# Results scattered by token rows and read back by plain loads, overflow blocks ahead of expert 29, roots and roundings of ScalarE ahead at the seam

## The reference, cut to what matters

```python
g_idx = argmax(xt @ w_gr + b_gr)                       # one of 4 groups per token
top_v, top_i = top_k(e_logits_of_that_group, 2)        # 2 of its 8 experts
wts = g_prob * softmax(top_v)
for each expert e of 32:                               # its tokens, xb
    y = (silu(xb @ w_gate[e]) * (xb @ w_up[e])) @ w_down[e]
h = h + sum over the token's two experts of wts * y    # 1024 result rows in all
h = rms_norm(h, final_gain)                            # then adaln and the convolution mixer
```

## Time and profile before

| | |
|---|---|
| time, median of 3 runs | 1503.96 us (1501.43 to 1504.95) |
| the profiled execution, its own time | 1503.66 us |
| its span, first to last instruction | 1501.9 us |
| mean granted TensorE clock | 0.985 |
| PE busy | 1409.8 us (94%) |
| DVE, ACT, POOL busy | 699.5, 486.0, 43.5 us |
| expert stage, first `up` to last `result` | 275.5 to 756.0 us |
| seam, PE without its own work until | 779.5 us |

### The profile page before, as it was taken

How to read it: one execution, slowest core, us unless ns; L and a number is a source line. 1 busy time by engine, 2 the same in 40 slices (tenths; PEclk the granted TensorE clock), 3 DMA queues, 4 the chain that set the end, 5 groups by cost and what they waited for, 6 DMA issues and landing times.

```text
span 1501.9 us, 18075 instructions
## 1 busy us (share of the span) xinstructions
PE 1409.8 (94%) x6944; PEld 984.8 (66%) x6944; DVE 699.5 (47%) x1311; ACT 486.0 (32%) x739; POOL 43.5 (3%) x75
## 2 busy tenths in 40 slices
PE   6999998999998888999859999999999999999997
PEld 5877677544433333343248888788888888888886
DVE  5377656611110111110077657466266566666555
ACT  6463335011100000111063221334344444444552
POOL 2001000000000000000120000000000000000000
PEclk9999899999999999999979999999999999999999
DMA  8827435699999998999985455202213122112101
GB/s 357 359 79 268 157 141 207 264 423 425 426 427 426 427 427 341 387 427 426 426 305 213 170 206 196 92 21 89 110 57 113 57 72 98 57 56 105 64 15 57
DMA packets 36809, 336.84 MB, mean 224 GB/s; under 512 B 4560, under 2 KB 4688, under 8 KB 18384
## 3 DMA queue, kind: packets, MB, share of 16 engines
q1 hardware_dynamic: 29632, 304.69, 50.3%
q0 software_dynamic: 6624, 29.89, 5.6%
q10 hardware_dynamic: 432, 0.60, 0.1%
HBM read 312.62 MB, written 22.54 MB: 223 GB/s over the span
## 4 chain that ended last, share of the span: by engine, by line
PE 81%; DMA 11%; DVE 4%; ACT 2%; issue 1%; SPq 0%; ACTq 0%; DVEq 0%
PE ps L342 79%; DMA ring<-in_wts_dram 7%; DMA ar<-in_wts_dram 3%; DMA y_scratch<-ar 1%; PE ps L852 1%; PE ps L672 0%; DVE hres L1940 0%; PE ps L362 0%; DVE ar L1502 0%; DMA hres<-in_x_dram 0%; DVE a_NL L1629 0%; DVE a_WL L1378 0%; DVE xlo L1696 0%; PE ps L576 0%; PE ps L353 0%
## 5 line engine op out<-in xcount | busy, mean ns | idle before, releaser
L342 PE MATMUL ps<-ring,ar 128*64 128x512 f32 x832 | 189.0, 600 | 20.7 <-issue 8.9
L1797 DVE TENSOR_TENSOR ar<-ar,ps 128x256 f32<-128x256 f32 x34 | 14.3, 422 | 355.6 <-ACT ar L1143 355.6
L342 PE MATMUL ps<-b_NH,b_WH 128*128 128x512 f32 (+1 forms) x688 | 175.8, 392 | 1.1 <-ACT b_NH L1009 1.1
L342 PE MATMUL ps<-b_NH,b_WL 128*128 128x512 f32 (+1 forms) x688 | 170.5, 385 | 0.0
L342 PE MATMUL ps<-ar 128*64 128x512 f32 (+5 forms) x782 | 162.3, 475 | 7.1 <-DVE ar L1566 2.4
L342 PE MATMUL ps<-b_NL,b_WH 128*128 128x512 f32 (+1 forms) x688 | 166.6, 385 | 0.0
L1378 DVE TENSOR_TENSOR b_WL<-ring,b_WH 128x1024 fp32r<-128x1024 f32 x104 | 127.0, 1221 | 75.2 <-ACT b_WH L951 75.2
L951 ACT ACTIVATE b_WH<-ring 128x1024 fp32r<-128x1024 f32 x104 | 110.0, 1057 | 124.9 <-PE ps L342 124.0
L342 PEld LDWEIGHTS ps<-ring,ar 128*64 128x64 f32 x832 | 60.8, 138 | 134.3 <-issue 116.4
L342 PEld LDWEIGHTS ps<-b_NH,b_WL 128*128 128x128 f32 x688 | 129.3, 188 | 25.8
L342 PEld LDWEIGHTS ps<-b_NL,b_WH 128*128 128x128 f32 x688 | 127.2, 188 | 25.5
(11 more groups left out here) (317 smaller groups left out, 1958.8 us busy)
## 6 DMA issues: line engine op xcount, KB each, us to landing
ring<-in_wts_dram SPq DMA_DIRECT2D x84, 2048.0 KB, 14.8
ar<-in_wts_dram SPq DMA_DIRECT2D x24, 2048.0 KB, 25.5
spare<-in_wts_dram SPq DMA_DIRECT2D x24, 2048.0 KB, 26.5
ring<-in_wmod_dram SPq DMA_DIRECT2D x24, 512.0 KB, 4.6
ar<-in_wmod_dram POOLq DMA_DIRECT2D x24, 512.0 KB, 3.9
y_scratch<-gate POOLq DMA_DIRECT2D x11, 1024.0 KB, 21.4
y_scratch<-gate SPq DMA_DIRECT2D x44, 128.0 KB, 24.8
y_scratch<-ar SPq DMA_DIRECT2D x24, 128.0 KB, 24.3
```

The source lines that it names most:

```text
L342: return pe.matmul(o, l, m, start=start, stop=stop, skip_group_check=True)
L1797: return dve.tensor_tensor(h.rearrange("p (a c) -> p a c", a=2), g_.rearrange("p (a c) -> p a c", a=2), ps[:, b, :].rearrange("p (a g c) - ...
```

## The change

- `y_scratch` has one row for each (token, choice), 1024 rows and one spare. POOL writes each expert's result with one indirect scatter DMA, half rows of 2 KB; rows of unused slots have an index out of bounds and are left out. An expert without a third block sends one scatter in which a single half row goes to the spare row. SP stores no results any more.
- The row index of each slot is computed on the way. PE multiplies the one-hot `OH` with a table `rid` (`rows_of_slots`, 4 matmuls for four experts) and turns the answer over the partitions (`turn_rows`, 8 small float32 matmuls); DVE copies and compares (`copy_rows`, `main_rows`). A third block does the same for itself (`rows_of_third`, `turn_rows_third`, `third_rows`).
- After the last scatter SP reads `y_scratch` with four plain loads of 1 MB. POOL's eight gathers are gone, and so are the eleven zero writes.
- The twelve overflow blocks stand ahead of expert K_OV = 29 in the programs of PE, ACT and DVE, with an `Else` that counts the semaphores on; on SP they stand ahead of n = 27, on POOL behind n = 28.
- At the seam ACT scales two of the four quarters of `hres` before `result(31)`, then does all four `hi`, then the other two quarters.

```diff
+            def rows_of_slots(g):
+                pe.wait_ge(S["i_dv"], 2 * g + 1)
+                for p in range(4):
+                    t = mm(ps[0:4, 3, 0:256], rid[:, p, :], OH[:, p, :], p == 0, p == 3)
+            def turn_rows(g):
+                pe.wait_ge(S["i_dv"], 2 * g + 2)
+                for u in range(4):
+                    v = ix_main[u // 2][:, (u % 2) * 64:(u % 2) * 64 + 64]
+                    for j in range(2):
+                        t = mm(ps[64 * j:64 * j + 64, 3, 256 + 2 * u:258 + 2 * u], v, coef, True, True)
...
             def main_pick(n):
                 if n + 4 < NE:
                     pe.wait_ge(S["m_oh"], n // 4 + 2)
+                    if n % 4 == 2:
+                        rows_of_slots(n // 4 + 1)
+                    if n % 4 == 3:
+                        turn_rows(n // 4 + 1)
+                    if n == 1:
+                        turn_rows(0)
...
             for n in range(NE):                       # PE; ACT and DVE alike
+                if n == K_OV:
+                    with pe.If(n_over > 0):
+                        for j in range(NOV):
+                            with pe.If(n_over > j):
+                                overflow(j)
+                            with pe.Else():
+                                no_overflow(j, 1)
+                    with pe.Else():
+                        no_overflow(0, NOV)
...
-            result(NE - 1)                            # ACT
-            hi(P_C0, 0)
             act.wait_ge(S["std"], 1)
-            for p in range(4):
+            for p in range(2):
+                rooted(p)
+            result(NE - 1)
+            for n in range(4):
+                hi(P_C0, n)
+            for p in range(2, 4):
+                rooted(p)
...
-                dve.wait_ge(s_yg[2 * p + c], 16)      # DVE, pick
+                dve.wait_ge(s_yg[p], 16)
...
-            pool.memset(gz, 0.0).then_inc(S["const"], 1)
-            for c in range(11):
-                pool.dma_start(yz[:, c * 2048:(c + 1) * 2048], gz).then_inc(S["yzero"], 16)
...
+            def spread(y, q, sem):                    # POOL
+                pool.indirect_dma_start(
+                    out=y_halves, out_offset=bass.IndirectOffsetOnAxis(ap=row_i[:, q:q + 1], axis=0), in_=y, in_offset=None,
+                    bounds_check=2048, oob_is_err=False).then_inc(S[sem], 16)
+            def main_out(n):
+                pool.wait_ge(S["m_y"], n + 1)
+                pool.wait_ge(S["i_dv"], 2 * (n // 4) + 3)
+                spread(ysb[n % 3], n, f"y{n % 3}")
-            for m in range(8):
-                pool.indirect_dma_start(out=yg[m], out_offset=None, in_=y_d, ...).then_inc(s_yg[m], 16)
...
-            def result_out(n):                        # SP
-                load_behind(n, 2)
-                sp.wait_ge(S["m_y"], n + 1)
-                store(n, ysb[n % 3], f"y{n % 3}")
+            for p in range(4):
+                sp.dma_start(yg2[p], y_tiles[:, p, :]).then_inc(s_yg[p], 16)
```

More of the change, by code:

```diff
@@ L18 @@
 NOV = 12
-NSLOT = (2 * NE + NOV) * CAP
+SKIP = 1 << 20
+K_OV = 29
+NT = NE + NOV
 RING = 4
@@ L83, in program @@
         s_slot = [ctx.enter_context(nc.semaphore(f"s_slot{j}")) for j in range(8)]
-        s_yg = [ctx.enter_context(nc.semaphore(f"s_yg{m}")) for m in range(8)]
+        s_yg = [ctx.enter_context(nc.semaphore(f"s_yg{m}")) for m in range(4)]
         same = ExitStack()
@@ L272, in program @@
         yg = [area(1024 * j, 1024) for j in range(8)]
+        yg2 = [area(2048 * p, 2048) for p in range(4)]
         fgr, fgsq = area(8192, 1024), area(9216, 1024)
@@ L763, in tensor_program @@
             down_main(NE - 1)
[L765 to L788, removed]
             pe.wait_ge(S["m_y"], NE)
-            pe.wait_ge(S["t_y"], NE)
+            pe.wait_ge(S["t_y"], NT)
             pe.wait_ge(S["hi"], cno(P_C0, 2) + 1)
@@ L1170, in scalar_program, with no_overflow @@
             n_over, third = read_ctl(act)
+            def no_overflow(j, k):
+                for v in ("t_xg", "t_sg", "t_ht", "t_y"):
+                    act.wait_ge(S[v], K_OV + j)
+                    act.sem_inc(S[v], k)
             for n in range(NE):
+                if n == K_OV:
+                    with act.If(n_over > 0):
+                        for j in range(NOV):
+                            with act.If(n_over > j):
+                                act.wait_ge(S["t_tx"], 3 * (K_OV + j))
+                                third_block(K_OV + j)
+                            with act.Else():
+                                no_overflow(j, 1)
+                    with act.Else():
+                        no_overflow(0, NOV)
+                v_ = turn_no(n)
                 if n:
@@ L1828, in vector_program @@
             slots_of_choices()
+            dve.wait_ge(S["pc"], 23)
+            behind()
+            signals(dve.tensor_tensor(X[:, 0:4, :], OO[:, 0:4, :], bc(mid(e64), 128, 4, 32), ALU.mult))
+            behind()
+            signals(dve.tensor_reduce(e0_f, X[:, 0:4, :], AX.X, ALU.add))
+            behind()
+            dve.tensor_copy(rid[:, :, 2], e0_f).then_inc(S["i_dv"], 1)
             for u in range(2, 4):
@@ new lines, in third_out @@
+            def third_out(u, sem):
+                pool.wait_ge(S["t_y"], u + 1)
+                pool.wait_ge(S["t_e"], 11 * u + 11)
+                spread(ysb3, 32, sem)
+            def main_out(n):
+                pool.wait_ge(S["m_y"], n + 1)
+                pool.wait_ge(S["i_dv"], 2 * (n // 4) + 3)
+                spread(ysb[n % 3], n, f"y{n % 3}")
+            for n in range(NE):
+                with pool.If(third(n)):
+                    third_out(turn_no(n), "ty")
+                with pool.Else():
+                    pool.wait_ge(S["i_dv"], 1)
+                    if n:
+                        pool.wait_ge(S["ty"], 16 * n)
+                    spread(f32(xhi[:, 0, 0:512]), 33, "ty")
+                if n == K_OV - 1:
+                    with pool.If(n_over > 0):
+                        for j in range(NOV):
+                            with pool.If(n_over > j):
+                                third_out(K_OV + j, "tyo")
+                if n < NE - 1:
+                    main_out(n)
@@ L2311, in sync_program @@
             n_over, third = read_ctl(sp)
-            def store(b, y, sem):
-                for q in range(2):
-                    sp.dma_start(y_d[b * CAP:(b + 1) * CAP, 512 * q:512 * q + 512],
-                                 y[64 * q:64 * q + 64, :]).then_inc(S[sem], 16)
             def load_behind(n, m):
@@ L2322, in load_behind @@
                         load(i)
-            def result_out(n):
-                load_behind(n, 2)
-                sp.wait_ge(S["m_y"], n + 1)
-                store(n, ysb[n % 3], f"y{n % 3}")
-            for n in range(NE):
-                with sp.If(third(n)):
-                    if n:
-                        result_out(n - 1)
-                    sp.wait_ge(S["t_up"], n + 1)
-                    load_behind(n, 0)
-                    load_behind(n, 1)
-                    sp.wait_ge(S["t_y"], n + 1)
-                    store(NE + n, ysb3, "ty")
-                with sp.Else():
-                    load_behind(n, 0)
-                    if n:
-                        result_out(n - 1)
-                    load_behind(n, 1)
-            result_out(NE - 1)
             def overflow(j):
```

276 lines of the change are left out of this document (191 added, 85 removed).

## The result

The changed kernel takes 1514.09 us in the median of six runs (1510.14 to 1515.21), the kernel before 1503.88 us in six runs beside it: a ratio of 1.0066, with a 95% interval from 1.0054 to 1.0078. Forecast was 1500.4 us, faster. It is slower, outside the range, and 2.7 us above the rival "PE's refill is more than one fetch" (1511.4 us). The profiled execution has a span of 1513.2 us against 1501.9, which makes 11.3 us to explain.

What follows compares the result with a forecast made beforehand. PE and DMA by turns bound the expert stage, then the seam. Last result -5.5 - 4.9 + 6.4 + 6.8 - 5.1 = -2.3 us, seam -1.0: from 1503.66 to 1500.4 us, own range 1497 to 1503.5, whole range 1492.5 to 1505.9.

Steps and rivals of the forecast that it cites:

- PE's refill is more than one fetch: Rival, chance 0.11: the jump at expert 29 empties PE's buffer, each further fetch costs 5.5 us; slower, 1511.4 us.
- DVE's row: DVE's 5.48 us gap at the seam before, read as instruction fetch; priced PE's jump at expert 29 at 6.8 us.
- Less to store: Expert stage: fewer stored bytes, 18 stores ahead of the landing at 549.40 save 0.31 us each, -5.5 us.
- Third blocks: Experts 19 and 20: scatters avoid SP's queue, so PE's idle and the slow clock behind it go, -4.9 us.
- Index work: PE behind 549.40: small matmuls for row indices and third blocks add 6.4 us, between 4.2 and 11.
- Tail: Last experts: 5.1 us of waiting for weights vanish, since PE is now later than they are.
- Seam: Last result to PE's first product: first pick starts at +9.3 against +10.3, gain 1.0 us, between -2 and +2.
- Early roots: Seam: ACT's two early roots fit, ending some 0.8 us before the last down, if DVE's 5.48 us are gone.
- The rival (+4.3): Chance 0.10: DVE's 5.48 us belong to expert 31's Else, so early roots hold the last result back; 1504.7 us.
- Behind the seam: From PE's first product at 779.50 to the end: nothing of the change is there, carried over unchanged.

## Why the prediction was wrong

**The step that failed** is "PE's code is far longer than DVE's, and its jump now stands between `main_turn(28)` and `up(29)` ... So I price it by DVE's row". It was right that the jump is a fetch, and that nothing covers it; the term was 6.8 us and measured 14.8: 12.4 of idle and 2.4 at and behind the low clock. The price of one fetch was nearly right: where only one counts, PE idles 5.8 to 7.2 us, for DVE's 5.5. What was missing is the second one. After the jump the packet of the target has to come, and the next one comes only 5.7 to 6.2 us behind it; if the target stands at the end of its packet, both lie bare. I had this as the rival with 0.11 and argued against it that PE streams its code without gaps elsewhere. That row says nothing of a jump: in the stream ahead of expert 29 two packets come 9.7 us apart (691.0 and 700.7 us) and PE never waits for one, but after the jump PE needs the next packet as soon as four instructions are done. The rival's own picture, block after block because code is issued fast, was not right either: in these runs it is at most two packets, and the layout decides whether it is one. That its 1511.4 us lie so near is luck: they stand for three fetches, and the last result and the stretch behind the seam make up for the one that did not come. Nor did it take 16 us of idle to be slower, as I had worked out: 12.4 were enough with the +2.7 of the last result and the +3.3 behind the seam, and with 32 instructions of padding and one fetch the kernel still took 1506.0 us in one execution, against 1502.5 for the kernel before beside it.

PE's own jump stood in the trace of the kernel before, and would have been a better row than DVE's. It is the `If` at line 785, hidden there behind the matmuls that PE had queued and the rest of the seam:

```profile
L785 PEldq COMPARE_BRANCH  x1: 5765/5765/5765, 751.8 to 751.8; - x1
```

It gives the one fetch, 5.8 us; nothing in that trace shows the second.

The Trainium skill, Runtime: NRT & Kernel Launch, section Instruction fetch mechanics, says that code comes in blocks of 16 KiB, 256 instructions. The traces agree: 1.39 MB in 85 packets are 16.4 KB each, and a shift by 256 changes nothing. By the same section PE has room for 2048 instructions, which by the prediction's count would let three blocks, some 550 instructions, pass without a stall; they cost 7 us. A note in the section speaks of two such blocks only, 512 instructions, and with that the runs agree: one overflow block, an estimated 180 instructions, passes and three don't.

**The terms in turn.**
- *Less to store*, -5.5: the landing at 549.40 moved to 547.23, -2.2. Left-out rows are not written: from 450 to 540 us six scatters of 256 KB and their six half rows move 0.70 MB in POOL's queue, where full ones would be 1.6. But the rate fell: the window 420:450 moved 421 GB/s against 427, and the three windows up to 540 423, 422 and 425 against 426, 426 and 428. Over these 120 us 0.9% is 1.1 of the missing 3.3 us; the rest stays open, and that the scatters lower the rate was not tested.
- *Third blocks*, -4.9: held. No release by a store, and 3.65 us in place of 5.35.
- *Index work*, +6.4: too high. -2.2, -4.9 and this term give -3.27 at expert 28, so it is 3.8 us. A `turn_rows` took 0.6 us, not 1.4, so 0.04 us for each of its 16 passes: below every row that I held it against, 0.17 for 128-column weights and 0.09 for the transposes. (The lower end that I gave, 2.4 us for three at half the price, should have been 2.05; three took 1.9.) The errors of the first and third term nearly cancel: -4.0 predicted, -3.3 measured.
- *Tail*, -5.1: held, to 0.03 us, for the reason given. In the versions without the stall the landing's wait is back.
- *Seam*, -1.0: held (-1.04), in part by luck. The scatter had landed 3.1 us after the result and not 4.0, a time for which no row stood, so the first `pick` came at +8.4 and not at +9.3; the third then waited 0.98 us for its megabyte.
- *Early roots*: the forecast let them fit, at no cost, and they cost 2.7 us. The rival (+4.3) had the right place, too high a price and the wrong mechanism. I let DVE's sums take 1.2 us each, as before, and never asked what stood beside them. Before, POOL's sums ran from 747.17 to 751.83 us and DVE's began at 756.27, behind its jump; now they run from 756.46 to 761.13, and DVE's begin at 757.46.
- *Behind the seam*, 0 predicted, +3.3, most of it at the low clock. Over all versions the stretch from PE's first product to the end is 722.4 to 725.7 us, and the repeats of three kernels agree within 0.5 us, so it belongs to the kernel. What decides it stays open.

## What to carry to other kernels

On this kernel's PE a branch over much code is a fetch of 6 to 7 us in the open, or two, however little is executed. Put such a branch where the engine is idle anyway, and read how long the branch instruction takes in the trace, and when the instruction queue brings its packets, before you price it. When the stall sits at 12 rather than 6 us, padding the untaken code by part of a packet, and then by a whole one, tells whether the layout is to blame. When work is moved beside an engine's instructions, look up what those instructions last with a neighbour, not alone.

## What the runs showed of the hardware

- PE after a jump over 3 to 12 blocks: idle for 5.8 to 7.2 us for one packet of 16.4 KB, 11.7 to 12.6 us when the landing is at the packet's end (six profiles), over traffic at some 420 GB/s. A jump over one block was nearly free (0.88 us of idle, 0.52 without any).
- DVE and POOL adding two float32 tiles of 128x1024 at once: DVE's two take 5.89 us (4.76 and 1.21), alone 2.33. POOL's two, begun 1.0 us earlier, take 4.67 beside DVE and 4.68 alone; here it is DVE that pays.
- An indirect scatter holds POOL for 0.97 us and had landed 2.33 us after its start at the seam.
- Four plain loads of 1 MB from one queue: 9.8 us in the median, and a 512 KB load of another queue ahead of the second one delays it by 1.2 us.
